# Factors spread over the partitions by transpositions of a broadcast column instead of products with the identity

## The chip, the cores and the metric
The kernel runs on one core of one Trainium2 chip. The metric is the device time of one execution in microseconds (us). TensorE (PE in the profile, PEld for its weight loads) does the matmuls and writes PSUM banks of 128 partitions x 512 fp32 columns; VectorE (DVE), ScalarE (ACT) and GpSimd (POOL) do the rest, and SyncE (SP) issues the weight DMAs.

## What is computed
Two transformer blocks on a sequence of 512 tokens of width 1024, batch 1. Cut to what matters here:

```python
def rmsnorm(x, g):                       # over the channels of each token
    y = xf * lax.rsqrt(jnp.mean(xf * xf, axis=-1, keepdims=True) + EPS)
    return y * g

# first block
h = rmsnorm(x, g1);  p, q, k, v = split(h @ w_in)
o = diff_attention(...)                  # 4 heads; each head's output is rmsnorm-ed
x = x + concat(pool(p), o) @ w_o
x = x + (silu(gate) * val) @ w_down      # gate, val = conv(rmsnorm(x, g2) @ w_up)
x = rmsnorm(x, g3)
# second block
h = x + 0.5 * rmsnorm(swiglu(rmsnorm(x)))
u = rmsnorm(h) @ w_in2                   # 8-head attention over the top 128 keys of a token; softmax
                                         # HGRN2 recurrence with 4 heads, each rmsnorm-ed
h = h + rmsnorm(merged @ w_out)
h = h + 0.5 * rmsnorm(swiglu(rmsnorm(h)))
h = h + rmsnorm(sigmoid(rmsnorm(h) @ w_ple_gate) * (p @ w_ple_proj))
```

Every root mean square is one number per token, and so is every sum of a softmax.

## The kernel before
All activations lie transposed: channels on the 128 partitions, the 512 tokens along the free dimension, in tiles of 128x512. A weight matrix comes in units of up to 8 blocks of 128x128, through four slots (`raw`, filled by SP's DMA queue when the PE has finished the unit four before). ACT rounds each unit to `w_hi`, DVE or POOL makes the rest `w_lo`, and a product is three matmuls over 512 columns (w_hi with the activations' high and low part, w_lo with the high part), lines 801 to 803 and their copies 823 to 825, 897 to 899, 996 to 998, 1259 to 1261. Each output tile accumulates in a PSUM bank; banks 0 to 3 are for these, 4 to 6 for small products ("aux"), bank 7 (`stat_bank`) for statistics.

The order of work on each engine is written out by hand. The stages are: projections and attention of the first block, `wo`, `up1`, `down1`, `up2`, `down2`, projections of the second block (`proj2`) with the indexer's top-k, the attention over selected keys (a loop of 32 steps, 8 heads x 4 blocks of queries, with pieces of `proj2` filled in between), the HGRN levels, `branch`, `out`, `up3`, `down3`, `ple`.

A norm goes in four steps. The squares of the channels are summed to one tile `sum_sq`. `sum_columns` (line 839) multiplies each of its four 128x128 parts with a column of ones: a column of 128 sums, one token per partition. ACT takes the root (line 1376), DVE the reciprocal (`inverse`, line 1911): 128x4, one column for each 128 tokens. Now the factors lie one token per partition, but they are wanted along the free dimension and in all partitions. `spread` (line 865) does that: for each of the four columns it takes the column, broadcast to 128x128, as the stationary operand and the identity as the moving one; the product has the factor of token t in every partition of column t. After the fourth it raises `spread_ready`; DVE then copies the bank to `rstd` (line 1917) or scales with it directly (lines 1928, 2054, 2664).

There are 21 such spreads: norm1, four heads of the first attention, norm2, final1, pre1, post1, mixpre, ckv, kidx, four heads of HGRN, postmix, pre2, post2, plepre, plepost. The spread stands in the PE's queue where its bank and its factors are expected to be ready: between the two halves of a tile for norm1, norm2, final1, mixpre, pre2, plepre; right behind the sums, with nothing to do in between, for post1 and postmix. The four heads' spreads stand one behind the other, each in its own bank; DVE scales head h (line 1928), ACT rounds it (line 1390), DVE makes its low part (line 1943), and PE goes on with `wo` or `branch` on it.

The attention over selected keys does the same for each head's softmax sums (lines 1171 to 1174): the reciprocals `key_factors(h)` (line 2502) go to `stat_bank`, ACT copies them to `rstd` (line 1707), and DVE scales the head's output (line 2514). That is 8 more spreads, in every fourth step of the loop, behind the step's filling and ahead of its products with the latent values (line 1178). A step's other work there: the logits (PE line 1148, DVE line 2489 with a bias mask that POOL makes at line 768 from `t_bias`, which ACT's queue loads), the exponentials (ACT line 1693), the transpositions of the probabilities (PE line 1155), and their copy (ACT line 1685).

Transpositions by `pe.transpose(out, in_, identity)` are there already, of data that is not broadcast: v (line 984), the first attention's probabilities (line 1044), ckv (line 1118), i (line 1130) and line 1155.

Of the kernel before, what the change touches and what calls it, by code (L numbers as in the profile page):

```python
# [38 lines left out]
P = 128  # L39
# [302 lines left out]
def two_blocks(nc, ins, spill, bias_rows, out):  # L342

    with ExitStack() as ctx:
# [33 lines left out]
        ident = keep("ident", [P, P])  # L378
# [5 lines left out]
        inverse = keep("inverse", [P, 4 * QB])  # L384
# [125 lines left out]
        stat_bank = bank[7]  # L510

        def tile_bank(stage, i):
            return bank[TILE[stage, i][0]]
# [8 lines left out]
        def tile_read(stage, i):  # L522
            return tile_sem(stage, i), TILE[stage, i][1] + 1
# [7 lines left out]
        def norm_of(name):  # L531

            group, h = name[:-1], name[-1]
            if group in ("head", "hgrn"):
                return group, QB * int(h), bank[BANKS + int(h)]
            return name, QB * (name == "pre1"), stat_bank
# [8 lines left out]
        def key_factors(h):  # L545

            return inverse[:, QB * (2 + h % 2):QB * (3 + h % 2)]
# [9 lines left out]
        def aux_read(*name):  # L557
            return aux_sem(*name), AUX[name] // AUX_BANKS + 1
# [220 lines left out]
        def _(pe):  # L779
            mm = nc.tensor.matmul  # L780

            def wait(pair):
                pe.wait_ge(pair[0], pair[1])

            def wait_bank(stage, i, turn=0):

                number, former = TILE[stage, i]
                if former:
                    pe.wait_ge(bank_free[number], former + turn)
# [39 lines left out]
            def aux_wait(*name):  # L829

                n = AUX[name]
                if n >= AUX_BANKS:
                    pe.wait_ge(aux_free[n % AUX_BANKS], n // AUX_BANKS)
                return bank[BANKS + n % AUX_BANKS]
# [8 lines left out]
            def stat_bank_free(name):  # L843
                if STAT[name]:
                    pe.wait_ge(rstd_ready, STAT[name])
# [19 lines left out]
            def spread(name):  # L865

                group, column, dst = norm_of(name)
                pe.wait_ge(inverse_ready, SUM[group] + 1)
                if group == name:
                    stat_bank_free(name)  # L870
                for j in range(QB):
                    step = mm(dst[:, j * P:(j + 1) * P], inverse[:, column + j:column + j + 1].broadcast_to([P, P]),  # L872
                              ident[:, :], start=True, stop=True)
                step.then_inc(spread_ready, 1)

            def aux_all_free(n):
# [3 lines left out]
            def total_x(name):  # L880
                sum_x(name)
                spread(name)
# [130 lines left out]
            for a in range(ATT_STEPS + 2):  # L1013
# [6 lines left out]
                if a < ATT_STEPS:  # L1020
                    h, i = a // QB, a % QB
# [3 lines left out]
                    for n, dst in enumerate(scores):  # L1025
                        rows = slice(64 * n, 64 * n + 64)
                        mm(dst[:, 0:end], q1[rows, HEADS - 1 - h, i * P:end], k1[rows, h, 0:end], start=True,
                           stop=False)
                    for dst in scores:
                        mm(dst[:, end - 64:end], neg_row[0:1, :], one_row[0:1, :], start=False,  # L1030
                           stop=True).then_inc(aux_ready, 1)
# [8 lines left out]
                if 1 <= a <= ATT_STEPS:  # L1040
                    dst = aux_wait("turn", a - 1)
                    pe.wait_ge(attn_ready, a)
                    for j in range((a - 1) % QB + 1):
                        step = pe.transpose(dst[:, j * P:(j + 1) * P], attn[:, (a - 1) % 2, j * P:(j + 1) * P],
                                            ident[:, :])
                    step.then_inc(aux_ready, 1)
                if a < 2:
                    dst = aux_wait("bias", a)
                    cols = slice(0, T) if a == 0 else slice(T, BIAS_COLS)
                    mm(dst[0:DSA_HEADS, 0:cols.stop - cols.start], rel[:, :], onehot[:, cols], start=True,  # L1050
                       stop=True).then_inc(aux_ready, 1)
                if a in POOL_AT:
                    g = POOL_AT[a]
                    dst = aux_wait("pool", g)
                    pe.wait_ge(pool_ready, POOL_ORDER.index(g) + 1)
                    mm(dst[:, :], pool_w[:, g, :], pool_d[:, g % 2, :], start=True, stop=True).then_inc(aux_ready, 1)
                if a >= 2:
                    b = a - 2
                    h, i = b // QB, b % QB
# [4 lines left out]
                    dst = tile_bank("attn", h)  # L1064
                    for j in range(i + 1):
                        step = mm(dst[:, i * P:(i + 1) * P], v1[:, j, h, :], attn_t[:, b % 2, j * P:(j + 1) * P],
                                  start=(j == 0), stop=(j == i))
# [27 lines left out]
            for n in range(LEAD2):  # L1095
# [4 lines left out]
                for kind, m in AFTER2[n]:  # L1100
# [6 lines left out]
                    elif kind == "wturn":  # L1107
                        dst = aux_wait(kind, m)
                        wait(tile_read("proj2", 2))
                        for j in range(QB):  # L1110
                            step = pe.transpose(dst[:, j * 8:j * 8 + 8], widx_t[0:8, j * P:(j + 1) * P],
                                                ident[0:8, 0:8])
                        step.then_inc(aux_ready, 1)
                    elif kind == "ckvtok":
                        dst = aux_wait(kind, m)
                        pe.wait_ge(norm_ready, 1)
                        for j in range(QB):
                            step = pe.transpose(dst[:, j * P:(j + 1) * P], ckv[:, j * P:(j + 1) * P], ident[:, :])
                        step.then_inc(aux_ready, 1)
                    elif kind == "qlat":  # L1120
                        dst = aux_wait(kind, m)
# [3 lines left out]
                           stop=True).then_inc(aux_ready, 1)  # L1125
                    elif kind == "vturn":
                        dst = aux_wait(kind, m)
                        wait(tile_read("proj2", 11 + m))
                        for j in range(QB):
                            step = pe.transpose(dst[:, j * P:(j + 1) * P], i_t[:, m % 2, j * P:(j + 1) * P],  # L1130
                                                ident[:, :])
                        step.then_inc(aux_ready, 1)
                    else:
                        dst = aux_wait(kind, m)
                        i, h = IDX_STEPS[m]
# [6 lines left out]
            for a in range(DSA_STEPS + 4):  # L1142
                if a < DSA_STEPS:
                    h, i = a // QB, a % QB
                    end = (i + 1) * P
                    dst = aux_wait("logit", a)
                    wait(aux_read("qlat", h))
                    mm(dst[:, 0:end], qlat[:, h, i * P:end], ckv[:, 0:end], start=True,
                       stop=True).then_inc(aux_ready, 1)
                if 2 <= a < DSA_STEPS + 2:  # L1150
                    b = a - 2
                    dst = aux_wait("turn2", b)
                    pe.wait_ge(exp2_done, b + 1)
                    for j in range(b % QB + 1):
                        step = pe.transpose(dst[:, j * P:(j + 1) * P], prob2[:, b % 4, j * P:(j + 1) * P],
                                            ident[:, :])
                    step.then_inc(aux_ready, 1)
                fill("proj2", FILL2[a])
                if 3 <= a < DSA_STEPS + 3:
                    b = a - 3  # L1160
                    h, i = b // QB, b % QB
                    if i == 0:
                        wait_bank("olat", h)
                        wait(aux_read("ckvtok", 0))
                    if i == QB - 1:
                        pe.wait_ge(sums_inverted, h + 1)
                        if h:
                            pe.wait_ge(factors_kept, h)
                        else:
                            pe.wait_ge(rstd_ready, STAT["kidx"] + 1)  # L1170
                        for j in range(QB):
                            step = mm(stat_bank[:, j * P:(j + 1) * P], key_factors(h)[:, j:j + 1].broadcast_to([P, P]),
                                      ident[:, :], start=True, stop=True)
                        step.then_inc(factors_ready, 1)
                    wait(aux_read("turn2", b))
                    dst = tile_bank("olat", h)
                    for j in range(i + 1):
                        step = mm(dst[:, i * P:(i + 1) * P], ckv_tok[:, j, :],
                                  attn2_t[:, b % 2, j * P:(j + 1) * P], start=(j == 0), stop=(j == i))
                    if i == QB - 1:  # L1180
                        step.then_inc(head_ready, 1)
                if a in YA_AT:
                    t = YA_AT[a]
                    dst = aux_wait("ya", t)
                    wait(tile_read("olat", 2 * t))
                    wait(tile_read("olat", 2 * t + 1))
                    for n in range(2):
                        step = mm(dst[64 * n:64 * n + 64, :], wuv[:, 2 * t + n, :], olat[:, n, :], start=True,
                                  stop=True)
                    step.then_inc(aux_ready, 1)  # L1190
# [18 lines left out]
            for h in range(HEADS):  # L1209
                s = h % 2  # L1210
                dst = aux_wait("pair0", h)
                pe.wait_ge(k_ready, h + 1)
                for j in range(QB):
                    cols = slice(j * P, (j + 1) * P)
                    step = mm(dst[:, cols], hk[:, s, cols], hq[:, s, cols], start=True, stop=True)
                step.then_inc(aux_ready, 1)
                for l, b in enumerate(LEVELS):
                    e = h * len(LEVELS) + l
                    dst = aux_wait("pair", h, l)
# [3 lines left out]
                    if l == 0:  # L1223
                        for j in range(QB):
                            half = slice(j * P // 2, (j + 1) * P // 2)
                            step = mm(dst[:, half], hk[:, s, j * P:(j + 1) * P], chunk[:, s, half], start=True,
                                      stop=True)
                    elif b <= 64:
                        for j in range(QB):
                            block_ = pairs[:, j * P:(j + 1) * P]  # L1230
                            to = dst[:, j * P // 2:(j + 1) * P // 2].rearrange("p (n c) -> p n c", c=b)
                            step = mm(to, block_, block_.rearrange("p (n c) -> p n c", c=2 * b)[:, :, b:2 * b],  # L1232
                                      start=True, stop=True)
                    else:
                        pieces = ([(0, P, P, 0), (2, 3 * P, P, P)] if b == 128 else
                                  [(0, 2 * P, 2 * P, 0), (1, 2 * P, 2 * P, 2 * P)])
                        for j, q0, n, col in pieces:
                            step = mm(dst[:, col:col + n], pairs[:, j * P:(j + 1) * P], pairs[:, q0:q0 + n],
                                      start=True, stop=True)
# [48 lines left out]
            for i in range(DC):  # L1288
                dst, u = tile_bank("pproj", i), UNIT["pproj"][0] + i // 4
# [8 lines left out]
                for c in range(2):  # L1298
# [4 lines left out]
                    step = mm(dst[:, :], wl, p_split[:, c, :], start=False, stop=(c == 1))  # L1303
# [1469 lines left out]
```

## Time and profile before
| | |
|---|---|
| time, median of 3 runs | 1907.04 us (1906.33 to 1907.34) |
| the profiled execution: its span, first to last instruction | 1902.0 us |
| what lies around the span (median of the runs less the span; the profiled execution's own time isn't listed) | 5.0 us |
| PE busy | 1833.2 us (96% of the span), 8472 matmul instructions |
| DVE, ACT, POOL busy | 57%, 35%, 11% |
| mean granted clock of TensorE | 0.993 |

A matmul's busy time is not what it occupies the engine for: matmuls are pipelined, and a row with count 8 and a length of 1.05 us is followed by the next instruction 0.81 us after its start. Distances between starts are what an edit can save. The clock is given as a share of 2.4 GHz.

### The profile page before, as it was taken

To read this page: it belongs to the slowest core of one execution; us is meant where nothing else is said; L and a number is where in the kernel's file an instruction comes from. 1 tells how busy PE (TensorE), PEld (TensorE's weight loads), DVE (VectorE), ACT (ScalarE), POOL (GpSimd) and SP (SyncE) were. 2 spreads that over 40 slices of the span, in tenths; PEclk is the share of its full clock that TensorE was granted. 3 is DMA by queue.
4 is the path that set the end of the run, shared out by engine and by line. 5 is a ranking of instruction groups with operands and counts; after the bars stand their busy time and mean duration, and the time that the engine had idled before them with its cause. 6 is when DMAs were issued, how large, how long until landed. Compare 5 with 4: busy or idle time off the path is not lost.

```text
span 1902.0 us, 23891 instructions
## 1 busy us (share of the span) xinstructions
PE 1833.2 (96%) x8472; PEld 1483.5 (78%) x8472; DVE 1088.5 (57%) x1658; ACT 665.1 (35%) x1010; POOL 208.0 (11%) x272
## 2 busy tenths in 40 slices
PE   6998999999999999999989998999998999999989
PEld 4676888888888888888776776789776888888866
DVE  6565588887334654532252676587665655552265
ACT  5333333333233222222243334565453322232244
POOL 2332000000000000000024445433000000000000
PEclk9999999999999999999999999999998999999999
DMA  4677232223222222233222233232341322233211
GB/s 157 61 85 44 90 113 96 99 99 110 91 98 78 99 90 98 99 106 99 93 71 74 95 128 122 73 106 78 114 147 56 100 99 99 94 119 103 83 67 66
DMA packets 55460, 180.63 MB, mean 95 GB/s; under 512 B 6336, under 2 KB 7104, under 8 KB 55392
## 3 DMA queue, kind: packets, MB, share of 16 engines
q1 hardware_dynamic: 43344, 157.33, 24.6%
q10 hardware_dynamic: 12048, 22.40, 7.5%
q8 instruction: 41, 0.67, 0.1%
q14 instruction: 27, 0.22, 0.0%
HBM read 167.65 MB, written 12.06 MB: 94 GB/s over the span
## 4 chain that ended last, share of the span: by engine, by line
PE 83%; DVE 9%; DMA 3%; ACT 3%; issue 2%; POOL 0%; ACTq 0%; SPq 0%; DVEq 0%
PE bank L801 20%; PE bank L803 20%; PE bank L802 20%; PE bank L823 2%; PE bank L825 2%; PE bank L824 2%; DMA raw<-in_w_proj 2%; PE bank L897 2%; PE bank L898 2%; PE bank L899 1%; DVE score L2399 1%; DVE best L2398 1%; PE bank L872 1%; PE bank L839 1%; PE bank L1232 1%
## 5 line engine op out<-in xcount | busy, mean ns | idle before, releaser
L1341 ACT ACTIVATE w_hi<-raw 128x1024 fp32r<-128x1024 f32 (+2 forms) x281 | 304.5, 1087 | 734.2 <-PE bank L803 625.9
L801 PE MATMUL bank<-a_hi,w_hi 128*128 128x512 f32 x1192 | 466.4, 391 | 3.3 <-DVE gate L2383 2.7
L803 PE MATMUL bank<-a_hi,w_lo 128*128 128x512 f32 x1192 | 464.0, 389 | 0.0
L802 PE MATMUL bank<-a_lo,w_hi 128*128 128x512 f32 x1192 | 463.8, 389 | 0.0
L1957 DVE TENSOR_TENSOR w_lo<-raw,w_hi 128x1024 fp32r<-128x1024 f32 (+2 forms) x222 | 284.0, 1280 | 255.2 <-ACT w_hi L1341 241.8
L801 PEld LDWEIGHTS bank<-a_hi,w_hi 128*128 128x128 f32 x1192 | 223.7, 188 | 57.9 <-issue 7.7
L715 POOL TENSOR_TENSOR w_lo<-raw,w_hi 128x256 fp32r<-128x256 f32 x196 | 150.5, 801 | 1019.6 <-ACT w_hi L1341 1019.6
L803 PEld LDWEIGHTS bank<-a_hi,w_lo 128*128 128x128 f32 x1192 | 223.7, 188 | 47.0
L802 PEld LDWEIGHTS bank<-a_lo,w_hi 128*128 128x128 f32 x1192 | 223.8, 188 | 45.8
L801 PE MATMUL bank<-h_hi,w_hi 128*128 128x512 f32 x528 | 205.4, 389 | 0.0
L802 PE MATMUL bank<-h_lo,w_hi 128*128 128x512 f32 x528 | 205.4, 389 | 0.0
L803 PE MATMUL bank<-h_hi,w_lo 128*128 128x512 f32 x528 | 205.4, 389 | 0.0
L803 PEld LDWEIGHTS bank<-h_hi,w_lo 128*128 128x128 f32 x528 | 99.1, 188 | 20.7
L802 PEld LDWEIGHTS bank<-h_lo,w_hi 128*128 128x128 f32 x528 | 99.1, 188 | 20.6
L801 PEld LDWEIGHTS bank<-h_hi,w_hi 128*128 128x128 f32 x528 | 99.1, 188 | 20.5
L823 PE MATMUL bank<-a_hi,w_hi 128*128 128x512 f32 x250 | 108.3, 433 | 0.0
L825 PE MATMUL bank<-a_hi,w_lo 128*128 128x512 f32 x250 | 99.0, 396 | 0.0
L824 PE MATMUL bank<-a_lo,w_hi 128*128 128x512 f32 x250 | 98.6, 394 | 0.0
L2316 DVE TENSOR_TENSOR val<-bank,rstd 128x512 f32<-128x512 f32 x44 | 30.4, 691 | 113.9 <-PE bank L803 113.9
L897 PE MATMUL bank<-a_hi,w_hi 128*128 128x512 f32 x150 | 64.0, 427 | 30.9 <-DVE a_lo L1963 29.5
L897 PEld LDWEIGHTS bank<-a_hi,w_hi 128*128 128x128 f32 x150 | 30.1, 201 | 44.3 <-DVE a_lo L1963 28.8
L898 PE MATMUL bank<-a_lo,w_hi 128*128 128x512 f32 x150 | 61.7, 411 | 0.0
(330 smaller groups left out, 2343.2 us busy)
## 6 DMA issues: line engine op xcount, KB each, us to landing
raw<-in_w_up SPq DMA_DIRECT2D x132, 512.0 KB, 3.4
raw<-in_w_down SPq DMA_DIRECT2D x48, 704.0 KB, 4.1
raw<-in_w_proj SPq DMA_DIRECT2D x59, 512.0 KB, 3.5
raw<-in_w_wo SPq DMA_DIRECT2D x8, 512.0 KB, 3.5
raw<-in_w_branch SPq DMA_DIRECT2D x16, 256.0 KB, 2.7
gates_in<-spill ACTq DMA_DIRECT2D x16, 256.0 KB, 2.9
raw<-in_w_out SPq DMA_DIRECT2D x8, 512.0 KB, 3.9
raw<-in_w_ple SPq DMA_DIRECT2D x8, 512.0 KB, 3.5
```

Source lines behind the costliest of these rows:

```text
L715: made = pool.tensor_tensor(lo[:, part], src[:, part], hi[:, part].bitcast(F32), ALU.subtract)
L801: mm(dst[:, :], wh, hi[:, k, :], start=(first and c == 0), stop=False)
L802: mm(dst[:, :], wh, lo[:, k, :], start=False, stop=False)
L803: step = mm(dst[:, :], wl, hi[:, k, :], start=False, stop=(last and c == n - 1))
L823: mm(dst[:, :], wh, a_hi[:, c, :], start=(c == 0), stop=False)
L824: mm(dst[:, :], wh, a_lo[:, c, :], start=False, stop=False)
L825: step = mm(dst[:, :], wl, a_hi[:, c, :], start=False, stop=(c == DC - 1))
L897: mm(dst[:, :], wh, hi[:, k, :], start=(k == 0), stop=False)
L898: mm(dst[:, :], wh, lo[:, k, :], start=False, stop=False)
L1341: fn(w_hi[:, slot, 0:size], raw[:, slot, 0:size], ACT.Copy).then_inc(unit_high, 1)
L1957: v.tensor_tensor(w_lo[:, slot, 0:size], raw[:, slot, 0:size], w_hi[:, slot, 0:size].bitcast(F32), ALU.subtract).then_inc(unit_split, 1)
L2316: v.tensor_tensor(val[:, :], bank[u][:, :], rstd[:, :], ALU.mult).then_inc(bank_free[u], 1)
```

## The change
Both places where a column of factors is spread use `pe.transpose` instead of a matmul. Operands, banks, waits, semaphores and order stay as they are.

```diff
@@ spread(name), norm and head factors
                 for j in range(QB):
-                    step = mm(dst[:, j * P:(j + 1) * P], inverse[:, column + j:column + j + 1].broadcast_to([P, P]),
-                              ident[:, :], start=True, stop=True)
+                    step = pe.transpose(dst[:, j * P:(j + 1) * P],
+                                        inverse[:, column + j:column + j + 1].broadcast_to([P, P]), ident[:, :])
                 step.then_inc(spread_ready, 1)
@@ attention over selected keys, the factors of a head
                         for j in range(QB):
-                            step = mm(stat_bank[:, j * P:(j + 1) * P], key_factors(h)[:, j:j + 1].broadcast_to([P, P]),
-                                      ident[:, :], start=True, stop=True)
+                            step = pe.transpose(stat_bank[:, j * P:(j + 1) * P],
+                                                key_factors(h)[:, j:j + 1].broadcast_to([P, P]), ident[:, :])
                         step.then_inc(factors_ready, 1)
```

## Rows read from the trace of the kernel before

**Rows 1.** The page: busy us of each engine, share of the span, instructions.
```profile
PE 1833.2 (96%) x8472; PEld 1483.5 (78%) x8472; DVE 1088.5 (57%) x1658; ACT 665.1 (35%) x1010; POOL 208.0 (11%) x272
```

**Rows 2.** Groups of instructions by shape: count, busy us and mean ns, idle before.
```profile
L872 PE MATMUL bank<-ident,inverse 128*128 128x128 f32 x168 | 22.2, 282 | 3.2 <-DVE inverse L1911 3.2
L1155 PE MATMUL bank<-ident,prob 128*128 128x128 f32 x80 | 14.4, 278 | 6.2 <-ACT prob L1693 4.8 <-DVE logit L2489 0.8 <-ACT attn_t L1685 0.6
```

**Rows 3.** Line 1172's own view: ns min/median/max, first and last start.
```profile
L1172 PE MATMUL bank<-ident,inverse x64: 271/275/275, 1169.2 to 1242.6; 128*128 128x128 f32 x64
```

**Rows 4.** Timeline of PE around the spread of norm1: start and length in us.
```profile
35.73 1.05 PE L872 MATMUL bank<-ident,inverse 128*128 128x128 f32 x8
36.54 0.48 PE L823 MATMUL bank<-a_hi,w_hi 128*128 128x512 f32 x1
```

**Rows 5.** Timeline of PE around four transpositions, in three settings.
```profile
1050.46 0.60 PE L1130 MATMUL bank<-ident,i_t 128*128 128x128 f32 x4
1050.82 0.48 PE L801 MATMUL bank<-a_hi,w_hi 128*128 128x512 f32 x1
...
115.91 0.60 PE L1044 MATMUL bank<-ident,attn 128*128 128x128 f32 x4
116.34 0.83 PE L1066 MATMUL bank<-attn_t,v 128*128 128x128 f32 x6
...
1176.01 0.66 PE L1155 MATMUL bank<-ident,prob 128*128 128x128 f32 x4 [0.77 <-DVE logit L2489]
```

**Rows 6.** The chain that ended last: two of its twenty stretches of spreads, one of sums.
```profile
1004.47 1.16 PE bank L872 x8
1233.14 0.89 PE bank L1172 x8
1439.74 1.80 PE bank L839 x16
```

**Rows 7.** Timeline of PE and DVE at the four heads of the first attention.
```profile
182.99 3.73 PE L872 MATMUL bank<-ident,inverse 128*128 128x128 f32 x32
184.08 0.75 DVE L1928 SCALAR_TENSOR_TENSOR chunk<-o,par,bank 128x512 f32<-128x512 f32 x1 [3.26 <-PE bank L872]
185.05 0.75 DVE L1928 SCALAR_TENSOR_TENSOR chunk<-o,par,bank 128x512 f32<-128x512 f32 x1 [0.21 <-PE bank L872]
186.69 0.50 PE L996 MATMUL bank<-mix_hi,w_hi 128*128 128x512 f32 x1
186.74 0.75 DVE L1928 SCALAR_TENSOR_TENSOR chunk<-o,par,bank 128x512 f32<-128x512 f32 x1
```

**Rows 8.** Timeline behind the spread of norm2: what DVE and PE do next.
```profile
241.99 0.69 DVE L1917 COPY rstd<-bank 128x512 f32<-128x512 f32 x1
255.91 0.50 PE L801 MATMUL bank<-a_hi,w_hi 128*128 128x512 f32 x1 [0.33 <-DVE w_lo L1957]
```

**Rows 9.** The chain that ended last, in the attention over selected keys.
```profile
1167.87 7.24 DMA t_bias<-bias_rows
1244.20 0.61 ACT rstd L1707
```

**Rows 10.** Stretches: busy us of PE, PEld, DVE, ACT, POOL, clock, DMA share, GB/s.
```profile
1442.00:1453.00 11.00, 7.31 (x22) 5.84 (x22) 8.10 (x14) 3.72 (x6) 0.00 (x0) 0.53 0.07 26
1480.00:1815.00 335.00, 335.00 (x1480) 277.37 (x1479) 150.24 (x175) 86.55 (x98) 0.00 (x0) 1.00 0.29 97
1176.00:1245.00 69.00, 68.23 (x413) 54.99 (x414) 36.53 (x93) 38.05 (x94) 30.79 (x39) 1.00 0.22 68
```

**Rows 11.** Timeline of PE at the lower clock: postmix, and two transpositions at 1161.
```profile
1442.20 1.81 PE L872 MATMUL bank<-ident,inverse 128*128 128x128 f32 x8 [0.68 <-DVE inverse L1911]
1448.06 0.63 PE L898 MATMUL bank<-a_lo,w_hi 128*128 128x512 f32 x1
1448.49 0.63 PE L899 MATMUL bank<-a_hi,w_lo 128*128 128x512 f32 x1
1161.35 0.63 PE L1155 MATMUL bank<-ident,prob 128*128 128x128 f32 x2
```

## The prediction
> **What bounds the kernel now.** I read the page first: the PE is busy for 96% of the span and DVE for 57% [rows 1], so whatever shortens the PE's queue should count, unless it lies just ahead of a wait. Then the groups by shape and the view of one line, for the two lines that change. The reader should look at the counts. 21 spreads of 4 products are 84 products, yet line 872 has 168 instructions, and line 1172 has 64 for 32 products: an fp32 product of 128x128 is two instructions. Line 1155 transposes 8 heads x (1+2+3+4) = 80 blocks and has 80 instructions: a transposition is one. A single instruction takes the same in all, 282 and 275 against 278 ns [rows 2, 3], so the gain, if any, is in the count. Last I read the chain that ended last, to see which spreads are on it: 20 stretches, of which two hold four heads each. They cover 20 of the 21 spreads of line 872 (all but norm2) and six of the eight of line 1172; one of either is shown [rows 6].
>
> **The price of one spread.** Busy times overlap, so I take distances between starts. The spread of norm1 starts at 35.73 and the product behind it at 36.54: 0.81 us [rows 4]. In front of a narrow fp32 product the chain gives it 0.89 us [rows 6]. Four transpositions in the same two settings: 1050.82 - 1050.46 = 0.36 us ahead of a wide product, 116.34 - 115.91 = 0.43 us ahead of a narrow one [rows 5]. So a spread gives 0.45 or 0.46 us, a little over half. Where the PE stood idle before it, the spread lasts 1.16 us (kidx) [rows 6], and four transpositions after such a wait 0.66 us [rows 5]: 0.50 us, which is also how much earlier its result is there. The operands are on the same sides (identity moving; column or data as weights). The one difference to the existing transpositions is that the column is broadcast, and the present spreads load just that as weights at no visible extra, so I take the plain transposition's price. Bounds: nothing gained if a broadcast column is dearer, 0.81 us if a spread cost nothing.
>
> The Trainium skill ("TensorE: Matmul & The Clock Gate", section Terms) says that the transpose mode makes fp32 four times faster. The trace doesn't agree for these sizes: 0.81 against 0.36 us is 2.2 times [rows 4, 5]. By the rule a spread would fall to 0.20 us and give 0.61; over the 20 spreads that count below, that is 3.2 us more than my sum.
>
> **What of it reaches the end.** Place by place:
> - Single spreads in front of work that the PE has in hand, or of DVE work that waits for the result: norm1, final1, pre1, mixpre, pre2, post2, plepre, plepost. All are on the chain. 8 x 0.45 = 3.6 us. For pre2, DVE's own chain of weight splits could have taken over, but the PE waits for nothing between 1480 and 1815 (335.0 of 335 us busy [rows 10]), so there is slack to run earlier into. norm1 is the least sure: the attention behind it waits for weight DMAs as well, but these are issued when the PE finishes a unit, so they move along.
> - Spreads after an idle PE, with DVE or the PE hanging on them: post1, ckv, kidx, 3 x 0.50 = 1.5 us. postmix starts as the clock falls: it lasts 1.81 us [rows 11], and the clock of its stretch is 0.53 [rows 10]. Two transpositions at the lower clock last 0.63 us [rows 11]; as one alone takes 0.42 of it by my estimate (0.63 less the one more start of some 0.21, half a wide product's 0.43), four last 0.42 + 3 x 0.21 = 1.05: 0.8 us.
> - norm2: nothing. DVE takes its result at 241.99 with no idle time before, coming straight from a weight split, and at 255.91 the PE waits for DVE [rows 8]. The 0.45 turns 0.33 us of wait into 0.78.
> - The four heads, twice. Today DVE starts on head 0 at 184.08, 1.09 us after the first product; it waits 0.21 us more for head 1, and the PE gets its first operand at 186.69 [rows 7]. With transpositions head 0's factors come 0.45 us earlier and head 1's are there before DVE asks: 0.45 + 0.21 = 0.66 us. The other two spreads give nothing, because from there DVE and ACT set the pace; the PE, which now reaches the products at 186.69 with hardly a wait, will stand idle for about 1.1 us. HGRN's heads are laid out alike: 2 x 0.66 = 1.3 us, where all eight in full would have been 3.6.
> - The softmax factors of eight heads: six on the chain, with the PE busy for 68.2 of the 69 us from 1176 to 1245 [rows 10]: 6 x 0.455 = 2.7 us. Head 0 gives nothing: its spread at 1169.2 [rows 3] lies inside the load of t_bias, which the chain follows for 7.24 us from 1167.87 [rows 9]. Head 7 neither: its last instruction starts at 1242.6 [rows 3], and ACT, occupied elsewhere, copies the factors only at 1244.20 [rows 9].
>
> Sum: 3.6 + 1.5 + 0.8 + 0 + 1.3 + 2.7 = 9.9 us, from 8 + 3 + 1 + 0 + 2 + 6 = 20 spreads. The span goes from 1902.0 to 1892.1. The runs' median is 5.0 us above the span of before, so the time goes from 1907.0 to 1897.1. No DMA, wait or instruction of another engine is added or moved; 116 matmul instructions go (8472 to 8356), and as many weight loads.
>
> **Rivals.**
> - *Clock lost at the heads.* Behind each block the PE will have done about 1.8 us of transpositions and stand idle for 1.1, where it did 3.6 us of products. Before postmix it summed for 1.80 us [rows 6] and stood idle 0.68, and the clock fell to its lower level, 1.2 GHz, for some 10 us [rows 10, 11]. If it falls behind the heads too, a wide product takes 0.43 us (starts 1448.06 and 1448.49 [rows 11]), so the six on one head need 2.6 us where DVE brings a head every 1.7 (185.05 to 186.74 [rows 7]): about 2 us lost in each block. Time 1899 for one, 1901 for both. For it: the likeness to postmix. Against: transpositions may hold the clock as products do.
> - *Slower than before: transpositions don't hold the clock.* If it then fell where products kept it, each fall in front of dense work would cost half its length; with some 10 us as at postmix, up to 5 us. Two such falls use up the sum of 9.9, and the third makes the kernel slower: 1912. Against: from 1176 to 1245 line 1155 puts transpositions into every step, and the clock stays at 1.00 [rows 10]. The Trainium skill (same page, section "Part 4: PE-mode transpose") says that the full clock does not engage for transposes. By that rule this rival would be the case; the trace disagrees as far as mixed work goes, and has no run of transpositions as long as the 16 of the heads.
> - *Absorbed in the loop over selected keys.* There DVE, ACT and POOL take turns with long latencies, and the PE did wait 0.77 us once [rows 5]. If their chain sets the loop, the 2.7 us vanish: 1899.8. Against: in six of the heads the chain goes through the spread itself.
> - *More than forecast.* All 29 in full are 25 x 0.45 + 1.5 + 0.8 = 13.5 us, 1893.5: that needs slack in DVE and the loads where I see none, or transpositions that are four times as fast.
> - *The change does nothing.* A broadcast operand might be transposed at the price of the product: 1907.0. Nothing in the trace speaks for it.
>
> **How the numbers follow.** Forecast as worked out, 1896 to 1898.5: 0.54. Clock at the heads: 0.14. Absorbed in the loop: 0.12. More: 0.10. Nothing: 0.05. Clock lost in general: 0.05. The time is that of the likeliest, 1897.1. The range reaches over more, absorption and the heads' clock: 1893.8 to 1901.3. A change within 0.2% (3.8 us, 1903.2 to 1910.9) is about what a measurement here can't tell from none. Forecast, heads' clock, absorption and more are faster, and so is a little of the last case, where one fall leaves a gain: 0.91. Same holds the case of nothing and two falls: 0.06. Slower, three or more falls: 0.03.
>
> **What would show it.** The two lines with 84 and 32 instructions of some 275 ns; a spread 0.36 us long from start to start; DVE at head 1 without a wait for the PE; about 1.1 us of wait before the first product on the heads; the wait near 255 at about 0.8 us; the clock at 1.00 behind both blocks of heads. The prediction is wrong if a spread's length isn't 0.36 to 0.43 us, if the clock falls where it held before, or if line 1155 or 1178 waits in the loop for what line 1172 has given.

## The result, and the profile after

| | median of the runs, us | span of the profiled execution, us |
|---|---|---|
| before | 1906.68 (4 runs, 1903.70 to 1907.34) | 1902.0 |
| after | 1894.99 (4 runs, 1893.82 to 1895.19) | 1892.8 |

The ratio is 0.9944, 95% interval 0.9933 to 0.9956: 0.0056 x 1906.68 = 10.7 us faster, between 8.4 and 12.8. Between the two profiled executions the span fell by 9.2 us (9.3 from the timelines).

The page of the kernel after, busy us of each engine, share of the span and instructions. To be held against [rows 1]: PE has 116 instructions and 11.9 us of busy time less, the others have the same counts.
```profile
PE 1821.3 (96%) x8356; PEld 1469.0 (78%) x8356; DVE 1089.7 (58%) x1658; ACT 665.9 (35%) x1010; POOL 207.6 (11%) x272
```
Its groups by shape: count, busy us and mean ns, idle before. As against [rows 2], the counts are halved and one instruction is 3 to 5 ns shorter than before (277 and 272 ns).
```profile
L872 PE MATMUL bank<-ident,inverse 128*128 128x128 f32 x84 | 12.0, 277 | 3.2 <-DVE inverse L1911 3.2
L1172 PE MATMUL bank<-ident,inverse 128*128 128x128 f32 x32 | 4.8, 272 | 0.0
```
The timeline of the kernel after at five places, with PE and DVE: norm1, norm2, the four heads of the first attention, a head of the loop over selected keys, and postmix.
```profile
35.54 0.60 PE L872 MATMUL bank<-ident,inverse 128*128 128x128 f32 x4
35.90 0.47 PE L823 MATMUL bank<-a_hi,w_hi 128*128 128x512 f32 x1
...
182.77 1.91 PE L872 MATMUL bank<-ident,inverse 128*128 128x128 f32 x16
183.40 0.75 DVE L1928 SCALAR_TENSOR_TENSOR chunk<-o,par,bank 128x512 f32<-128x512 f32 x1 [2.81 <-PE bank L872]
184.36 0.75 DVE L1928 SCALAR_TENSOR_TENSOR chunk<-o,par,bank 128x512 f32<-128x512 f32 x1 [0.21 <-PE bank L872]
186.00 0.50 PE L996 MATMUL bank<-mix_hi,w_hi 128*128 128x512 f32 x1 [1.33 <-DVE mix_lo L1943]
...
255.39 0.50 PE L801 MATMUL bank<-a_hi,w_hi 128*128 128x512 f32 x1 [0.79 <-DVE w_lo L1957]
...
1175.95 0.60 PE L1172 MATMUL bank<-ident,inverse 128*128 128x128 f32 x4
1176.38 1.06 PE L1178 MATMUL bank<-attn_t,ckv_tok 128*128 128x128 f32 x8
...
1435.91 0.65 PE L872 MATMUL bank<-ident,inverse 128*128 128x128 f32 x4 [0.68 <-DVE inverse L1911]
```
The reader should see four things. A spread ahead of a wide product now lasts 35.90 - 35.54 = 0.36 us, ahead of a narrow one 1176.38 - 1175.95 = 0.43 us; these were 0.81 and 0.89 [rows 4, 6]. At the heads the 0.21 us before DVE's second scaling is still there, and the PE waits 1.33 us for its first operand, where it had no idle time [rows 7]. The wait near 255 us is 0.79 us, against 0.33 [rows 8]. Postmix's spread takes 0.65 us where it took 1.81 [rows 11].

The same kernel's stretches, busy us of PE, PEld, DVE, ACT and POOL, then the clock, the DMA share and GB/s. The first two are those behind the two blocks of heads; the clock is 1.00 in both. Of the stretches shown, the clock is lower only in the one from postmix on, as before, and less so (0.69, against 0.53 in [rows 10]). The kernel has other falls, with either form of the spread: over 40 to 60, 940 to 960 and 1130 to 1160 us the mean is below 1.00 here, and before it was below 1.00 over 40 to 60, 950 to 960 and 1150 to 1170 us.
```profile
182.00:187.00 5.00, 3.67 (x24) 3.06 (x24) 2.99 (x5) 1.43 (x3) 0.00 (x0) 1.00 0.18 10
1339.00:1345.00 6.00, 4.67 (x29) 3.73 (x27) 3.45 (x5) 1.89 (x3) 0.00 (x0) 1.00 0.07 25
1436.00:1447.00 11.00, 7.51 (x23) 5.89 (x24) 9.37 (x15) 3.76 (x7) 0.00 (x0) 0.69 0.04 15
```

**Where the time came from.** For every spread I took its start before less its start after: the lead. What the lead grows by from one spread to a later one is what the change gave in between. The second column of leads is a second profiled execution of the same kernel (the run "after again" below), so that one can see what repeats.

| from the start of ... to the start of ... | forecast, us | after | after again |
|---|---|---|---|
| norm1, first heads | 0.45 | 0.03 | 1.86 |
| first heads, norm2 | 0.66 | 0.31 | 0.46 |
| norm2, final1 | 0 | -0.05 | -0.04 |
| final1, pre1 | 0.45 | 0.45 | 0.45 |
| pre1, post1 | 0.45 | 0.43 | 0.46 |
| post1, mixpre | 0.50 | 0.31 | 0.49 |
| mixpre, ckv | 0.45 | -0.03 | 0.32 |
| ckv, kidx | 0.50 | 0.49 | 0.53 |
| kidx, head 0 of the loop | 0.50 | 0.71 | 0.27 |
| head 0 to head 7 | 2.7 | 3.95 | 3.95 |
| head 7, hgrn heads | 0 | -0.03 | -0.08 |
| hgrn heads, postmix | 0.66 | -0.47 | 0.43 |
| postmix, pre2 | 0.8 | 1.13 | 1.13 |
| pre2, post2, plepre, plepost, end | 4 x 0.45 | 0.45, 0.47, 0.46, 0.47 | 0.44, 0.41, 0.46, 0.47 |

With a lead of 0.19 us at the start of norm1 (0.38 in the second execution), "after" adds up to 9.27 and "after again" to 12.39 us. The difference of 3.1 us arises mostly ahead of the first heads (1.8) and from hgrn to postmix (0.9); the program is the same. The kernel before has one profiled execution here, so a row that moves by a few tenths of a us is not a price.

### The profile page after: what moved, and what is told of

It is laid out like the page before. It is cut to its first block, busy times and chain, and to the rows that moved or that the text cites. A ratio compares the mean times of both kernels' runs of the same rounds, so it can differ in the third digit from the quotient of the medians.

```text
span 1892.8 us, 23659 instructions
## 1 busy us (share of the span) xinstructions
PE 1821.3 (96%) x8356; PEld 1469.0 (78%) x8356; DVE 1089.7 (58%) x1658; ACT 665.9 (35%) x1010; POOL 207.6 (11%) x272
## 4 chain that ended last, share of the span: by engine, by line
PE 82%; DVE 10%; ACT 3%; DMA 2%; issue 2%; ACTq 0%; POOL 0%; SPq 0%; DVEq 0%
PE bank L801 20%; PE bank L802 20%; PE bank L803 20%; PE bank L823 3%; PE bank L825 2%; PE bank L824 2%; DVE score L2399 2%; PE bank L897 2%; PE bank L898 1%; PE bank L899 1%; DVE best L2398 1%; DMA raw<-in_w_proj 1%; PE bank L839 1%; PE bank L1148 1%; PE bank L1232 1%
```

## The experiments

Four questions are put: what each group of spreads gives by itself; what an instruction costs in the queue; whether transpositions hold the clock; and whether the places forecast at nothing give nothing. To be free of what the first attention does by chance, I also give the time from DVE's reciprocal of the first four heads (before it starts at 180.57) to the end. It is 1721.47 us before, 1712.43 after and 1711.32 in "after again". I call it the time behind the heads; it holds every spread but that of norm1.

**Only the loop over keys** ("keys only"). Of the diff, only the second hunk is applied, line 1172.

> Only the softmax factors of the eight heads over selected keys are spread by transpositions; the norm spreads stay products. Prediction's account (six of eight count): 2.7 us less than before. Every spread counts in full: 3.6 us less. The loop is set by DVE, ACT and POOL: no change. The trace of the changed kernel suggests seven (the first head's gain is kept, the last one's isn't): 3.1 us less. Starts in the loop should gain 0.45 us on the kernel before with each head.

Measured: 1901.52 us (7 runs, 1899.63 to 1902.84), ratio 0.9973 (0.9962 to 0.9985) to 1906.38 of before, so 5.1 us (2.9 to 7.2). The time behind the heads is 1717.89, 3.6 us less. The timeline of this kernel in the loop, heads 0 and 1:
```profile
1171.00 0.60 PE L1172 MATMUL bank<-ident,inverse 128*128 128x128 f32 x4
1180.62 0.60 PE L1172 MATMUL bank<-ident,inverse 128*128 128x128 f32 x4
```
From head 0 to head 1 it takes 9.62 us, against 10.83 before (1169.17 to 1180.00), so this one head shows 1.21 us. That can't all be its spread: see the next two runs. The six spreads behind it gave 2.74 us, 0.46 each: from head 1 to head 7 it takes 59.07 us here and 61.81 before. The rival of absorption (a loss of all of the loop's gain) is out.

**Only the single spreads, or only the heads** ("single only", "heads only"). Line 872 is a transposition for one kind of spread, and line 1172 the product:
```
if group == name:      # single only; heads only: group != name
    step = pe.transpose(...)
else:
    step = mm(..., start=True, stop=True)
```

> Only the 13 single norm spreads are transpositions; the eight heads' spreads and the softmax factors stay products. Prediction's account: 8 x 0.45 + 3 x 0.50 + 0.8 + 0 for norm2 = 5.9 us less than before. In full: 6.4. If norm1's gain is lost in the first attention: 5.5.

> Only the two blocks of four heads are transpositions. Prediction: 0.66 us each, 1.3 us less than before. If the 0.21 us of DVE ahead of head 1 was not a wait for the PE but a fixed step: 0.45 each, 0.9 us. In full: 3.6 us. In every case but the last the PE then stands idle over 1 us ahead of the first product on the heads.

Measured: single 1897.49 (4 runs, 1896.05 to 1898.09), ratio 0.9950 (0.9933 to 0.9966), 9.5 us by the ratio and 5.9 behind the heads. Heads 1903.84 (10 runs, 1901.02 to 1905.80), ratio 0.9988 (0.9978 to 0.9998), 2.3 us by the ratio and 2.5 behind the heads. The three parts behind the heads are 3.6 + 5.9 + 2.5 = 12.0 us, and the whole gives 9.0 to 10.2. By the ratios the parts come to 5.1 + 9.5 + 2.3 = 16.9 us, against 10.7 for the whole; the singles' 9.5 is the odd one, 3 us above their forecast in full, and stays unexplained, so I price nothing by these medians. The excess behind the heads is found twice in the timelines of these kernels. With products in the loop, head 0 to head 1 takes 10.07 us in "heads only" and 10.36 in "single only", against 10.83 before: 0.5 to 0.8 us that no edit to this spread made. And in "heads only" the spread of postmix, still of products, met the fall of the clock later. In its timeline:
```profile
182.22 1.91 PE L873 MATMUL bank<-ident,inverse 128*128 128x128 f32 x16
185.46 0.50 PE L1000 MATMUL bank<-mix_hi,w_hi 128*128 128x512 f32 x1 [1.33 <-DVE mix_lo L1947]
...
1439.62 1.16 PE L876 MATMUL bank<-ident,inverse 128*128 128x128 f32 x8 [0.68 <-DVE inverse L1915]
```
The products of postmix take 1.16 us, not 1.81 [rows 11], and the stretch from there to pre2 is 0.6 us shorter (31.14 us against 31.75) without an edit there. So sums of parts are good to about 1 us each here. What "heads only" shows of its own part is the 1.33 us wait once more, and nothing slower than before: no clock was lost.

**Each transposition twice** ("twice"). It repeats work: each block is transposed twice, with the same values.
```
-                for j in range(QB):
+                for j in [*range(QB), *range(QB)]:
```
in both spreads of the kernel after, so that the PE has as many instructions as before the change.

> The changed kernel with the four transpositions of every spread done twice over (the same values written again), 116 more instructions. At 0.109 us each, a spread gets 0.44 us longer. If the places count as in the prediction (20 of 29 spreads, the heads only by their first): 8.7 us more than the changed kernel, so about 2 to 3 us less than before. If every spread counts: 12.7 us more, level with before or a little slower. If a spread's price isn't in its instructions but in the handover: hardly more than the changed kernel.

Measured: 1904.43 us (10 runs, 1903.75 to 1908.96), ratio 0.9993 (0.9983 to 1.0003). Behind the heads it is 1722.23, 0.8 us more than before and 9.8 more than after: all that the change gave is gone. My account expected 8.7 more. Of the 9.8, the stretch from head 0 to head 1 has 2.1 (11.76 us against 9.62), which is more than its spread's 0.44; the load of t_bias is on the chain there. Its timeline at norm1:
```profile
35.51 1.03 PE L872 MATMUL bank<-ident,inverse 128*128 128x128 f32 x8
36.30 0.48 PE L823 MATMUL bank<-a_hi,w_hi 128*128 128x512 f32 x1
```
Eight transpositions last 0.79 us, as eight instructions of products did (0.81 [rows 4]). A transposition's weight load is shorter than a product's (137 ns in the median here, 190 before, in the views of line 872), but at the same number of instructions that shows as 0.02 us a spread. What the change gives is the number of instructions, not a cheaper one.

**Does a long run of transpositions hold the clock?** ("hold transposes" and "hold products"). Both repeat work at one place, pre2, with the same values: 80 instructions in a row, of the one kind or of the other, ahead of dense work.
```
for j in list(range(QB)) * (20 if name == "pre2" else 1):    # transpositions
for j in list(range(QB)) * (10 if name == "pre2" else 1):    # products, two instructions each
```

> The changed kernel with pre2's spread done 20 times over: 80 transpositions one behind the other, 8.7 us at 0.109. If transpositions hold the clock as products do, the granted clock stays at 1.00 through them and the products behind start every 0.23 us. If they don't, the clock falls to 0.5 within them, their starts are 0.21 us apart from there, and the products behind begin 0.43 us apart.

> The changed kernel with pre2's spread made by products with the identity and done 10 times over: 80 instructions of 0.112 us, 8.9 us. The control of the run with 80 transpositions: the granted clock stays at 1.00 in either theory.

Measured, one run each: 1901.81 and 1903.83 us; behind the heads 1720.61 and 1720.41, so 8.2 and 8.0 more than after, and 9.3 and 9.1 more than "after again". The 76 instructions added are 8.3 us at 0.109. The first one's timeline and stretches (PE alone: busy, clock, DMA share, GB/s):
```profile
1473.69 0.48 PE L823 MATMUL bank<-a_hi,w_hi 128*128 128x512 f32 x1
1474.01 0.39 PE L824 MATMUL bank<-a_lo,w_hi 128*128 128x512 f32 x1
1474.24 0.40 PE L825 MATMUL bank<-a_hi,w_lo 128*128 128x512 f32 x1
...
1467.00:1470.00 3.00, 3.00 (x30) 1.00 0.00 1
1470.00:1473.00 3.00, 3.00 (x30) 1.00 0.00 0
1473.00:1476.00 3.00, 3.00 (x19) 1.00 0.03 5
```
and those of the second, with products:
```profile
1475.58 0.48 PE L823 MATMUL bank<-a_hi,w_hi 128*128 128x512 f32 x1
...
1469.00:1472.00 3.00, 3.00 (x30) 1.00 0.00 0
1472.00:1475.00 3.00, 3.00 (x30) 1.00 0.00 0
```
In 8.7 us of nothing but transpositions the granted clock stays at 1.00, and from the second on the wide products behind them follow each other every 0.23 us, as at full clock (0.43 at the lower [rows 11]). Products do the same. The two kernels differ by 0.2 us behind the heads. The rival "transpositions don't hold the clock" is refuted for a PE that was at full clock when they began; how they do on one at the lower clock wasn't tried. The Trainium skill ("TensorE: Matmul & The Clock Gate", section "Part 4: PE-mode transpose") says that the full clock does not engage for transposes; these runs don't agree.

**The change once more, and with work put behind the heads** ("after again" and "parts behind"). The first is the kernel after, unchanged. The second moves work of the PE from ahead of the four spreads to behind them, in the first attention and likewise in HGRN:
```
-            for at in range(HEADS):
+            for at in range(2):
                 out_part(3, at)
             aux_all_free(AUX_ATT)
             for h in range(HEADS):
                 spread(f"head{h}")
+            for at in range(2, HEADS):
+                out_part(3, at)
...
-            for c in range(4):
+            for c in range(2):
                 branch_part(2, c, 0)
             for h in range(HEADS):
                 spread(f"hgrn{h}")
+            for c in range(2, 4):
+                branch_part(2, c, 0)
```

> The changed kernel again, beside the others of this call: 10 to 12 us less than before on the same chip; the span of a profiled run 9 to 10 us less.

> The changed kernel with two of the four parts of the tile that stand ahead of each block of head spreads moved behind it (6 wide products, 1.38 us). If DVE and ACT set the pace from the first head on and the PE's idle 1.33 us there are free, the block starts 1.38 us earlier and the parts fill the idle time: 1.3 us less in each place, 2.6 us less than the changed kernel. If the time is given back where the PE waits for weight splits in the branch stage: 1.3 us less. If the factors aren't ready that early: no change.

Measured: after again 1894.09 us (5 runs, 1891.85 to 1894.51), ratio 0.9937 (0.9923 to 0.9950). Parts behind 1891.43 (5 runs, 1890.64 to 1892.65), ratio 0.9926 (0.9913 to 0.9940), with the same runs of before (1906.23). Behind the heads it is 1708.77, 2.6 us less than "after again", 3.7 less than after. Its timeline at the heads, and the two stretches (PE alone):
```profile
180.72 1.91 PE L872 MATMUL bank<-ident,inverse 128*128 128x128 f32 x16
181.36 0.75 DVE L1932 SCALAR_TENSOR_TENSOR chunk<-o,par,bank 128x512 f32<-128x512 f32 x1 [1.40 <-PE bank L872]
182.39 0.48 PE L996 MATMUL bank<-mix_hi,w_hi 128*128 128x512 f32 x1
...
182.00:187.00 5.00, 4.97 (x24) 1.00 0.08 6
1339.00:1345.00 6.00, 5.96 (x24) 1.00 0.00 0
```
DVE waits 1.40 us for the factors instead of 2.81, and the PE has no idle time before what follows them. The 1.33 us that stood open behind each block are used: 2 x 1.33 = 2.7, and 2.6 is what it gives. The medians are 2.7 us apart, but the intervals of the two ratios to before overlap (0.9923 to 0.9950 and 0.9913 to 0.9940), so this order is shown by one trace of each kernel and only likely by the runs. It is the best of the versions run.

**The places forecast at nothing, and the one in doubt** ("norm2 product", "norm1 product"). The kernel after, with this one spread left as products: `if name != "norm2":` (or `"norm1"`) ahead of the transposition, else the product.

> The changed kernel with norm2's spread alone back to products. Prediction: norm2's spread gives nothing, so the DVE starts behind 256 us stand, from there on, where they stood against the ones ahead of 240: no step there, and the PE's wait for the weight split near 255 falls from 0.78 to 0.33 us. If it counts: 0.45 us more from there to the end.

> The changed kernel with norm1's spread alone back to products. If norm1's 0.45 us pass through the first attention: 0.45 us more, too little to see in the median. If the loads of the first attention decide, the place of the heads' spreads against the changed kernel's moves by up to 2 us either way, as it does between two profiles of the changed kernel (182.8 and 180.8 us).

Measured: norm2 product 1893.94 us (4 runs, 1891.69 to 1894.93), ratio 0.9941 (0.9925 to 0.9957); norm1 product 1895.66 (5 runs, 1894.22 to 1897.43), ratio 0.9947 (0.9932 to 0.9962), before 1904.7. For norm2, the wait near 255 us in this kernel's timeline and in that of "after again":
```profile
253.12 0.50 PE L801 MATMUL bank<-a_hi,w_hi 128*128 128x512 f32 x1 [0.69 <-DVE w_lo L1961]
```
```profile
253.25 0.50 PE L801 MATMUL bank<-a_hi,w_hi 128*128 128x512 f32 x1 [0.81 <-DVE w_lo L1957]
```
Counted from the heads' reciprocal, the spread of final1, the next one, starts after 421.76 us with the slower spread of norm2, and after 421.60 and 421.78 in the two executions of the kernel after; behind the heads it is 1711.47, against 1711.32 and 1712.43. So norm2's form counts for nothing that these traces can show, as forecast. The wait itself missed my expectation of 0.33 us. From norm2's spread to where this wait begins it takes 14.69 us here as before, so the spread isn't the reason. What differs lies ahead: counted from the heads' reciprocal, norm2's spread starts 0.63 us earlier here than before (59.69 against 60.32 us), and the product behind the wait only 0.27 earlier (75.07 against 75.34). So in this trace the wait took up 0.36 us of what was gained ahead of norm2. In the two executions of the kernel after the gain ahead of norm2 passed the wait (0.30 and 0.29 us, 0.47 and 0.43). Why they differ in this isn't settled.

For norm1 it stays open. The first heads' reciprocal starts at 180.51 us in this kernel, at 180.34 in the one after and at 178.34 in "after again": the scatter of one kernel is 2.0 us, and 0.45 can't be seen in it. The traces of "norm2 product" and "hold products", whose program is the same up to there, have 178.05 and 181.26. What differs is in the waits of the first attention (us in all, count, longest), of the kernel after and of "after again":
```profile
ACT w_hi L1341 <- DMA raw<-in_w_proj: 13.0, 4, 5.9
```
```profile
ACT w_hi L1341 <- DMA raw<-in_w_proj: 10.5, 3, 4.7
```
ACT waits for the loads of the projection's weights for 2.5 us less in one execution than in the other. Why those loads land earlier isn't settled.

## Why the prediction was right

The forecast was 1897.1 us (1893.8 to 1901.3), and 1894.99 was measured: faster, in the range, 2.1 us under the value. The mechanism was right: fewer instructions in the PE's queue, counted only where a spread is on the chain. The closeness of the sum is in part luck, as the terms show. Point by point:

- **The price of a spread** was right: 0.36 and 0.43 us were forecast from existing transpositions, and 0.36 and 0.43 us are there. "Twice" shows why: time goes by instructions, about 0.1 us each, and a transposition is one where the product is two. The Trainium skill ("TensorE: Matmul & The Clock Gate", section Terms) says that the transpose mode makes fp32 four times faster, which by my estimate from 0.81 us would be 0.20; measured is 0.36, 2.2 times.
- **Singles** gave 0.41 to 0.47 us each at final1, pre1, pre2, post2, plepre and plepost, and ckv 0.49 and 0.53. The ones with a scatter are post1 (0.31 and 0.49; where it gave 0.31 the clock fell within its spread, which lasted 0.82 us against 0.65) and mixpre and kidx, whose stretches don't agree in the two executions: 0.68 and 0.59 together, where 0.95 was forecast. Norm1 is open.
- **Norm2** gained nothing, as forecast. The wait went from 0.33 to 0.79 (0.78 forecast). The control was less clean: with norm2's products back, the wait was 0.69 and not 0.33.
- **The heads** are a term that was too large: 0.66 forecast for a block. DVE started on head 0 at 183.40, 0.68 us earlier; less the lead of 0.22 us that the block began with, that is 0.46, and 0.31 to 0.46 of it reach norm2. The step that failed is "head 1's are there before DVE asks: 0.45 + 0.21". DVE did stand idle 0.21 us again before head 1 (183.40 to 184.36 is 0.96 us from start to start, 184.08 to 185.05 was 0.97 [rows 7]), though head 1's factors come four transpositions (0.44 us) behind head 0's, at about 183.40 + 0.44 = 183.84, and DVE ended its first scaling at 184.15. I had named "DVE at head 1 without a wait for the PE" as a sign to look for, and it didn't come; that the trace names the PE there is no sign of a wait on it. The gap is 0.21 us before, after, in HGRN and in "parts behind"; the code has DVE wait there for its own first scaling to be complete, which I argue is the cause, and no run took it away. The forecast wait of 1.1 us was 1.33, and that is what "parts behind" took up.
- **HGRN's heads** were forecast at 0.66 as well. The stretch up to postmix gave -0.47 in one execution and +0.43 in the other, and the traces show where they differ: one pair of ACT's issues of loads, at the same place in both, took 2.02 us in the first and 0.81 in the second, and ACT's next work had waited 1.44 us instead of 0.57 (the trace puts this wait down to DVE, which was done at 1371.19, 0.90 us before ACT went on). The first two lines are of the kernel after, the third is of "after again":
```profile
1370.02 2.02 ACTq L1745 DMA_DIRECT2D gates_in<-spill  x2
1372.09 1.34 ACT L1828 ACTIVATE gates_in<-gates_in,par 128x512 f32<-128x512 f32 x2 [1.44 <-DVE gates_in L2599]
1367.71 0.81 ACTq L1745 DMA_DIRECT2D gates_in<-spill  x2
```
  In before, "keys only" and "single only", whose heads are products, the stretch takes 95.12 to 95.16 us, and no such pair takes over 1.01 us. "Heads only", again without a long one, gains 0.48 on before; "hold transposes", with one of 1.87 us, loses 0.31. So HGRN's heads gave some 0.45 too, and slow issues took it back in some executions. Why an issue is slow isn't settled.
- **The loop over keys** is a term that was too small: 2.7 forecast, 3.95 measured from head 0 to head 7. Six heads gave their 0.455. Head 0, forecast at nothing since its spread "lies inside the load of t_bias", gave as well: head 0 to head 1 is 9.61 or 9.62 us in all eight traces that have the four transpositions there, against 10.07 in "heads only" with products, 0.45 apart. In those traces the chain runs through the spread, not the load, as in these lines of it from the kernel after:
```profile
1166.26 0.23 PE bank L825
1166.49 0.44 PE bank L1172 x4
1166.92 0.89 PE bank L1178 x8
```
  The load was on the chain again in "single only", where that stretch is 10.36 us, and in "twice", where it is 11.76:
```profile
1164.91 6.64 DMA t_bias<-bias_rows
1167.30 8.32 DMA t_bias<-bias_rows
```
  So 7 x 0.455 = 3.2, and the other 0.8 us (10.83 less 10.07) is when the load lands. The step that failed is "head 0 gives nothing: its spread lies inside the load": the load's landing moves from trace to trace, and I had taken it for a bound. I can't call it a mere accident either. It was on the chain in three of the four traces with eight instructions in each of the loop's spreads (6.6 to 8.3 us to land) and in none of the eight with four (5.9 us at most). Whether the change makes it land sooner isn't settled, so the 0.8 us has no shown cause. Head 7 gave nothing, as forecast: ACT's copy begins at 1237.42, 6.8 us before the 1244.20 of [rows 9], the lead head 7 already had.
- **Postmix** was forecast at 0.8 and gave 1.13, both times. The mis-sized step is the clock: at 0.65 us the four transpositions ran at full clock (0.66 after a like wait in [rows 5]), and not at the lower one that my 1.05 assumed. The fall came behind them. But only about half of the 1.13 is the edit: with products that too met the fall late ("heads only") the stretch takes 31.14 us, and 30.62 with transpositions, 0.52 less. The other 0.61 is where the clock fell in the one execution of before.
- **Around the span** I added 5.0 us. Each run's time is 2.1 to 2.2 us above its own span; the rest was that the profiled execution of before, at 1902.0 + 2.1 = 1904.1, was quicker than the median of its runs. Taken as it is, 1892.8 + 2.2 is the 1895.0 of after, while the median of before is 1906.7: that is how 9.3 us of span became 11.7 between the medians, with the ratio's 10.7 in between. Against the forecast of 1897.1, the span came out 0.7 us longer than the 1892.1 worked out, and the 5.0 was 2.8 us too much: the time lies 2.1 us under the forecast for this second reason. Between the profiled executions the change gave 9.3 us, less than the 9.9.

**The rivals.** *Clock lost at the heads*: refuted, 1.00 behind both blocks. *Transpositions don't hold the clock*: refuted by 80 in a row for a PE at full clock, and whole executions show no loss: the mean granted clock is 0.989 to 0.993 in the four runs of after and 0.987 to 0.993 in the 22 of before that stand beside "keys only". *Absorbed in the loop*: refuted by "keys only" and the 3.95. *All in full*, 1893.5: its time is closer to the result than the forecast's, but not its reason, since norm2, head 7 and all but the first spread of each block of heads gave nothing. *The change does nothing*: refuted. In all, the sum of 9.9 was held up by errors of both signs. In the execution after, the heads and the branch stage gave 1.5 us less than forecast (0.35 and 1.13), norm1, post1 and mixpre 1.1 less (0.42, 0.19 and 0.48), and the loop, the stretch ahead of it and postmix 1.8 more (1.25, 0.21 and 0.33).

## What to carry to other kernels

Count instructions, not operations: where the queue of the PE is full, an fp32 product with the identity that only moves data costs two instructions and a transposition one, and each spread on the chain gives that back in full. Where the PE runs into a wait behind the saved work, look for products that can be moved from ahead of the saved work to behind it: here the change left 1.33 us idle behind each block of heads, and moving two parts there took back 2.6 us. A transfer that is on the chain in one execution may not bind in the next, so a gain forecast at nothing behind a load deserves its full value as the upper bound.

## What the runs showed of the hardware

- 80 fp32 transpositions of 128x128 in a row took 0.109 us each and kept the full clock; 80 instructions of products took 0.112 us each. A broadcast column as the operand costs a transposition nothing (0.36 us for four, as with plain data).
- Between two scalings DVE stood idle for 0.21 us before and after the change, put down to the PE by the trace both times, though after it the factors were there some 0.3 us before DVE was free.
- The first attention of one and the same kernel ended 2.0 us apart in two executions, with waits for weight loads 2.5 us apart. With two more traces of the same program up to there it spans 3.2 us (178.05 to 181.26). A gain of less than that has to be read behind it.
- The spread of postmix, near which the clock falls in every trace, lasted 1.81 us or 1.16 us with the same eight instructions, as the fall came within it or behind it: 0.6 us of accident for any edit that shifts the work ahead.
- Two issues of loads on ACT's queue took 2.02 us in one execution and 0.81 in another at the same place of the same kernel, and the stretch around them was 0.9 us longer.
